# Attention of a streaming encoder step: value products in column strips, bounds inside the projections, the keys' scale moved to the queries

## The reference

```python
h = rms_norm(x, ln1)
proj = h @ w_in
q, k, v, f, xr, yg = jnp.split(proj, SPLITS, axis=-1)
q = rms_norm(q.reshape(B, T, N_HEADS, HEAD_DIM), q_gain)
k = rms_norm(k.reshape(B, T, N_HEADS, HEAD_DIM), k_gain)
...
s = jnp.einsum('bqhd,bkhd->bhqk', q, k) * ATTN_SCALE
s = s + cq - ck                       # cumulative log forget values
s = jnp.where(mask[None, None], s, -jnp.inf)
p = jax.nn.softmax(s, axis=-1)
return jnp.einsum('bhqk,bkhd->bqhd', p, v)
...
mixed = jnp.concatenate([rms_norm(attn, g_ao), rms_norm(lru_out, g_lo)], axis=-1)
x = x + mixed @ w_out
x = x + jnp.square(jax.nn.relu(rms_norm(x, ln2) @ w_up)) @ w_down
```

## Time and profile before

| | us |
|---|---|
| median of 3 runs (1530.29 to 1531.12) | 1530.82 |
| the profiled execution | 1526.91 |
| its span | 1525.2 |
| PE busy | 1423.7 |
| DVE busy | 735.3 |
| ACT busy | 421.4 |
| SP's transfers, share of 16 engines | 21.2% |

### The profile page before, as it was taken

The page is one execution under the profiler, slowest core; times in us unless marked ns, Lnnn a source line. Parts: engine busy times, 40 slices in busy tenths (PEclk is TensorE's granted clock), DMA queues, the critical chain, the costliest instruction groups (busy, mean ns, idle before and its releaser), DMA issues.

```text
span 1525.2 us, 19242 instructions
## 1 busy us (share of the span) xinstructions
PE 1423.7 (93%) x7499; PEld 1232.9 (81%) x7499; DVE 735.3 (48%) x1186; ACT 421.4 (28%) x741; POOL 83.2 (5%) x119
## 2 busy tenths in 40 slices
PE   4979989899898993998999999999999999999997
PEld 3765967859677882887989998999889988999896
DVE  6355364453634646675444454444444444444444
ACT  5124233242334546231312211221112211221110
POOL 2510101101000000000000000000000000000000
PEclk8989999999999996999999999999999999999999
DMA  6023432514222112111111110111011110111004
GB/s 186 8 69 91 127 79 68 143 44 120 65 75 68 30 57 94 60 42 47 60 32 55 41 41 28 55 55 41 19 50 55 41 41 28 55 41 44 24 28 125
DMA packets 133130, 92.87 MB, mean 61 GB/s; under 512 B 22358, under 2 KB 122710, under 8 KB 133076
## 3 DMA queue, kind: packets, MB, share of 16 engines
q1 hardware_dynamic: 133076, 92.14, 21.2%
HBM read 78.24 MB, written 9.68 MB: 58 GB/s over the span
## 4 chain that ended last, share of the span: by engine, by line
PE 88%; DVE 6%; ACT 2%; issue 1%; DMA 1%; POOL 1%; SPq 1%; ACTq 0%; DVEq 0%
PE psum L1473 25%; PE psum L1474 25%; PE psum L1475 25%; PE psum L1694 4%; PE psum L1678 1%; PE psum L1650 1%; DVE tops L1207 1%; PE psum L1681 1%; PE psum L1539 1%; PE psum L1772 1%; POOL rs L694 1%; PE psum L1586 1%; PE psum L1561 1%; DVE cross_qk L1199 0%; PE psum L1793 0%
## 5 line engine op out<-in xcount | busy, mean ns | idle before, releaser
L1441 DVE TENSOR_TENSOR mix<-psum,mix 128x512 f32<-128x512 f32 x288 | 196.4, 690 | 160.4 <-PE psum L1475 160.3
L1473 PE MATMUL psum<-h_hi,wu_hi 128*128 128x384 f32 x768 | 258.9, 337 | 4.2 <-DVE mix L1395 4.2
L1474 PE MATMUL psum<-h_lo,wu_hi 128*128 128x384 f32 x768 | 258.6, 337 | 0.0
L1475 PE MATMUL psum<-h_hi,wu_lo 128*128 128x384 f32 x768 | 258.6, 337 | 0.0
L1473 PE MATMUL psum<-wd_hi,u_hi 128*128 128x512 f32 x576 | 224.2, 389 | 3.6 <-issue 3.6
L1474 PE MATMUL psum<-wd_lo,u_hi 128*128 128x512 f32 x576 | 224.1, 389 | 0.0
L1475 PE MATMUL psum<-wd_hi,u_lo 128*128 128x512 f32 x576 | 224.1, 389 | 0.0
L1473 PEld LDWEIGHTS psum<-h_hi,wu_hi 128*128 128x128 f32 x768 | 144.9, 189 | 4.9 <-issue 4.4
L1474 PEld LDWEIGHTS psum<-h_lo,wu_hi 128*128 128x128 f32 x768 | 144.8, 189 | 0.5
L1475 PEld LDWEIGHTS psum<-h_hi,wu_lo 128*128 128x128 f32 x768 | 144.8, 189 | 0.0
L985 ACT CAST wd_hi<-raw 128x1024 fp32r<-128x1024 f32 x32 | 32.1, 1049 | 401.3 <-PE psum L1475 399.9
(11 more groups left out here) (257 smaller groups left out, 2137.3 us busy)
## 6 DMA issues: line engine op xcount, KB each, us to landing
raw<-in_w_up_dram SPq DMA_DIRECT2D x32, 512.0 KB, 4.6
raw<-in_w_down_dram SPq DMA_DIRECT2D x32, 512.0 KB, 3.3
k_c<-in_cache_k_dram SPq DMA_DIRECT2D x32, 256.0 KB, 3.0
raw<-in_w_in_dram SPq DMA_DIRECT2D x32, 192.0 KB, 4.1
out_dram<-mix SPq DMA_DIRECT2D x9, 512.0 KB
x_in<-in_x_prompt_dram SPq DMA_DIRECT2D x8, 512.0 KB, 4.0
v_c<-in_cache_v_dram SPq DMA_DIRECT2D x16, 256.0 KB, 4.9
kts<-in_cache_v_dram SPq DMA_DIRECT2D x16, 256.0 KB, 3.8
```

The costliest lines, as they stand in the source:

```text
L1441: nc.vector.tensor_tensor(at, psum[:, 4 + 2 * (t % 2) + half, :].rearrange("p (k n) -> p k n", n=P), at, ALU.add).then_inc(y_added, 1)
L1473: nc.tensor.matmul(out, hi(k), r_hi(k), start=first and k == 0, stop=False)
L1474: nc.tensor.matmul(out, hi(k), r_lo(k), start=False, stop=False)
L1475: last = nc.tensor.matmul(out, lo(k), r_hi(k), start=False, stop=end and k == n - 1)
```

## The change

**Steps and strips.** The steps of the two heads alternate. A pair of steps (the same tile of keys, head 0 and 1) has one `values(u)`: two float32 products with 64 columns of values each, into partitions 0 to 63 and 64 to 127 of one bank. The sums of the weights are products of their own, `weight_sums`: for four steps, four products with 32 columns of ones, into four strips of another bank. There are six `pt` buffers instead of three, laid over the buffer of cached values `v_c`, so those are loaded only when a pair's sums are done.

**Bounds.** The order of bounds is a table. Six of them, two turns of tops and the turn of tile 7 stand inside projections 7 and 8 or right behind them; `split_product` is cut into four quarters for that. High parts of tiles 4 and 5 are made after projection 6, of 6 and 7 at projection 8.

**The keys' gain.** The column with which queries are scaled is the product of both gains, so that keys are used without theirs. POOL multiplies the stored keys by the gain (`scale_keys`), after they were turned, and SP's stores wait for that.

**Smaller ones.** Two more small loads at the start; one copy of outputs per half instead of two; denominators copied whole; values are stored by one DMA; `share_out` moves from the projections into the attention.

```diff
 def attention_step(s):
-    if s < 8:
-        return s // 4, 0, s % 4
-    return (s - 8) // 8, 1, (s - 8) % 8
+    return (s % 2, 0, s // 2) if s < 8 else (s % 2, 1, (s - 8) // 2)
...
+    BOUND_AFTER = {(0, 2): ("b", 0, 0), (0, 3): ("b", 0, 1), (1, 0): ("b", 0, 3), (1, 1): ("s", 0, 0), (1, 2): ("b", 1, 0),
+                   (1, 3): ("b", 1, 1), (1, 4): ("s", 1, 0), (0, 5): ("b", 0, 4), (1, 5): ("b", 1, 4), (0, 6): ("b", 1, 5),
+                   (1, 6): ("b", 0, 6), (0, 7): ("b", 1, 6), (1, 7): ("b", 0, 7)}
...
     def bound_bank(hp, t):
-        return 6 + (5 * hp + t) % 2 if t < 4 else 6
+        if t < 4:
+            return 6 + (5 * hp + t) % 2
+        return 2 if (hp, t) in ((0, 4), (0, 5)) else 6
...
             for hp in range(2):
                 sp.dma_start(qgain[hp * DH:(hp + 1) * DH, :], q_gain.rearrange("a d -> d a")).then_inc(small_in, 16)
+                sp.dma_start(kgain_c[hp * DH:(hp + 1) * DH, :], k_gain.rearrange("a d -> d a")).then_inc(small_in, 16)
...
             def keys_out(p, t):
-                sp.wait_ge(qk_ready, NT * p + t + 1)
+                sp.wait_ge(k_scaled, NT * p + t + 1)
...
+                sp.wait_ge(den_done, 6 * p + 6)
+                past_values(p, 0)
                 if not last:
-                    sp.wait_ge(st_done, STEPS * (p + 1))
                     decay_rows(p + 1)
...
+                def scale_keys(t):
+                    pool.wait_ge(qk_turned, NT * p + t + 1)
+                    v = qk[:, t % 3, P:2 * P].rearrange("p (a d) -> p a d", d=DH)
+                    nc.gpsimd.tensor_tensor(v, v, kgain[:, None, :].to_broadcast([P, 2, DH]), ALU.mult).then_inc(k_scaled, 1)
+                    pool.wait_ge(k_scaled, NT * p + t + 1)
                 for t in range(NT):
                     pool.wait_ge(s4_ready, NT * p + t + 1)
                     nc.gpsimd.tensor_tensor(rs4[:, t % 2, :], m4[:, t % 2, :], neg_half[:], ALU.pow).then_inc(rs4_ready, 1)
+                    if t >= 1:
+                        scale_keys(t - 1)
+                scale_keys(NT - 1)
...
                 def exp(s):
                     act.wait_ge(st_done, STEPS * p + s + 1)
-                    if STEPS * p + s >= 3:
-                        act.wait_ge(pv_done, STEPS * p + s - 2)
+                    if s >= 6:
+                        act.wait_ge(den_done, 6 * p + (s - 6) // 4 + 1)
...
-                    d.link(nc.vector.tensor_tensor(v, psum[:, 4 + t % 2, 0:2 * P].rearrange("p (a d) -> p a d", d=DH),
-                                                   rs4[:, t % 2, :, None].to_broadcast([P, 4, DH]), ALU.mult))
-                    nc.vector.tensor_tensor(v[:, 2:4, :], v[:, 2:4, :], kgain[:, None, :].to_broadcast([P, 2, DH]),
-                                            ALU.mult).then_inc(qk_ready, 1)
+                    nc.vector.tensor_tensor(v, psum[:, 4 + t % 2, 0:2 * P].rearrange("p (a d) -> p a d", d=DH),
+                                            rs4[:, t % 2, :, None].to_broadcast([P, 4, DH]), ALU.mult).then_inc(qk_ready, 1)
...
                 for t in range(NT):
+                    if t == 5:
+                        low(0, 0)
+                        low(0, 1)
+                    if t == 7:
+                        bound(1, 1)
+                        bound(1, 2)
+                        bound(1, 3)
+                        bound(0, 4)
+                    if t == 8:
+                        bound(1, 4)
+                        bound(0, 5)
                     mean(t)
+                    if t == 8:
+                        bound(1, 5)
                     norm(t)
...
+                bound(0, 6)
                 low(4, 0)
+                bound(1, 6)
                 low(4, 1)
                 bound(0, 7)
+                bound(1, 7)
+                shift(0, 1)
+                shift(1, 1)
...
+                    for hp in range(2):
+                        r = head_rows(hp)
+                        last = nc.tensor.matmul(psum[r, 4 if qc == 0 else 0, a0 - qc * SPAN:SPAN], v1[:, kt, r],
+                                                pt[:, (s + hp) % 6, 0:a1 - a0], start=kt == 0, stop=kt == 4 * qc + 3)
+                    last.then_inc(pv_done, 1)
+                def weight_sums(kt_of):
+                    for i in range(4):
+                        s = 2 * kt_of + i
+                        _, qc, kt = attention_step(s)
+                        a0, a1 = step_queries(s)
+                        last = nc.tensor.matmul(psum[32 * i:32 * i + 32, 5 if qc == 0 else 1, a0 - qc * SPAN:SPAN], ones_s[:],
+                                                pt[:, s % 6, 0:a1 - a0], start=kt < 2, stop=kt >= 4 * qc + 2)
+                    last.then_inc(den_done, 1)
...
+                meanwhile = {0: (0, 6), 1: (1, 6), 2: (0, 7)}
+                for u in range(STEPS // 2):
+                    if u == 3:
+                        bound(1, 7)
+                    if u < STEPS // 2 - 1 and u != 3:
+                        scores(2 * u + 2)
+                        scores(2 * u + 3)
+                    values(u)
+                    if u % 2 == 1:
+                        weight_sums(u - 1)
+                    if u in meanwhile:
+                        bound(*meanwhile[u])
+                    if u == 3:
+                        turn_qk(NT - 1)
+                        turn_tops(0, 1)
+                        turn_tops(1, 1)
+                        scores(8)
+                        scores(9)
```

More of the change, by code:

```diff
@@ L526, in pair_transfers @@
                 duplicates(p, 0)
-                for t in range(5, NT):
+                for t in range(5, NT - 2):
                     keys_out(p, t)
@@ L1616, in project @@
                         pe.wait_ge(v_done, NT * p + t - 1)
-                    split_product(psum[:, 4 + t % 2, 0:PW3], lambda k: h_hi[:, k, tile(t)], lambda k: h_lo[:, k, tile(t)],
-                                  lambda k: wp_hi[:, k, :], lambda k: wp_lo[:, k, :], KC).then_inc(pair_proj, 1)
+                    for part in range(4):
+                        last = split_product(
+                            psum[:, 4 + t % 2, 0:PW3],
+                            lambda k: h_hi[:, 2 * part + k, tile(t)], lambda k: h_lo[:, 2 * part + k, tile(t)],
+                            lambda k: wp_hi[:, 2 * part + k, :], lambda k: wp_lo[:, 2 * part + k, :], 2, part == 0, part == 3)
+                        if part < 3:
+                            amid(t, part)
+                    last.then_inc(pair_proj, 1)
                 def turn_qk(t):
```

323 lines of the change are left out of this document (159 added, 164 removed).

## The result

The changed kernel takes **1551.55 us** (median of 4 runs, 1548.29 to 1554.80) against 1530.55 us for the kernel before in the same comparison: ratio 1.014, 95% interval 1.0125 to 1.0155. It is slower by 21 us, outside the forecast range of 1504 to 1531. About 7 of these 27.8 us come from the choice of executions: the one of before lies 3.6 us under its median, the one of the changed kernel 3.3 above its own. So against the forecast the medians miss by 31 us, the two profiles by 38.

The account below looks back on a forecast made before the run. Bound by PE, with time to win in the attention. Terms -24.4 (four pairs), +8.1 (clock), +4.7 (pair 0) and +1.2 (start) sum to -10.4 us, from 1530.82 to 1520.4 us; range 1504 to 1531.

Parts of the forecast that it names:

- The stretch of projections: From the streams' scores to the next pair's first score: +2.1 us for bounds, masks and turns, +1.0 for a late key load.
- The `k_c` waits: At turn_past(5), after the streams' scores: its load has 2.4 us of work to cover it instead of 3.4, +1.0 us a pair.
- The clause kept for the range: Loads for turn_past(6) and (7), queued behind 1 MB of values, might come late: +1 us a pair, not in the sum.
- Part A: Attention from the last projection's end to the second query half's first scores: 20.6 us becomes 13.9, -6.7 a pair.
- from there DVE's list runs: After bound(0, 6) at 4.4 us, DVE's maxima and low parts follow without a gap, ending at 10.8 us.
- Part B: Attention from the second query half's first scores to the streams' scores: 23.6 us becomes 21.1, -2.5 a pair.
- The clock: In the attention, PE's waits make its clock fall in three of four pairs, 2.7 us each: +8.1 us.
- Pair 0: Before the first bound: the store of key tile 4 waits for POOL and delays the forget rows, +4.7 us.
- The halves run one after the other: Rival on the attention's value products: 64-column halves run serially, +21 us for four pairs, 1533 to 1539 us; chance 0.13.
- It falls in all four, and the loads come late: Rival: PE's clock falls in all four pairs' attention and loads add up to 4 us, 1523 to 1527 us; chance 0.24.
- DVE clogs the last projections: Rival: maxima delay the norms, PE waits in projections 7 and 8, 1.5 to 2 us a pair, 1526 us; chance 0.10.
- The stores hold up the norms: Rival: norm(t + 3) waits for the late store of tile t's keys, 3 to 5 us a pair, 1530 to 1538; chance 0.05.

Follow-up runs that it names:

- the run with the moved store of pair 0: Changed kernel, with the store of key tile 4 in pair 0 alone placed behind the saving and loading of the forget rows: 1545.23 us.
- the last bound in banks of its own (and the turns moved): Changed kernel with all six edits of lists, POOL's order and turns, plus head 1's bound of tile 7 in the scores' two banks: 1513.80 us.
- DVE's low parts in its idle pieces: The last bound in banks of its own, plus ACT's third cache copy behind the last exponentials and DVE's low parts ahead of maxima: 1507.65 us.
- the version with the loads ahead: Changed kernel, with the load of the second group of cached values ahead of the store of key tile 1 in pairs 1 to 3: 1537.17 us.
- the version with the list edits alone: Changed kernel with three SP list edits: second group's values ahead of key tile 1's store, pair 0's store moved, first group's values behind last key loads: 1527.96 us.
- the version with the first group's values behind the keys: Changed kernel, with the first group's cached values (4 loads) behind the last two loads of keys in SP's list: 1540.26 us.

## Why the prediction was wrong

I forecast 1520.4 and measured 1551.55. In the profiles, where the miss is 38 us, 17 of it lie in the stretch of projections, by a term that I put at nothing (the loads behind the keys' store), and 19 in parts A and B, where the pace of DVE's list, the scores on PE and the base were mis-sized. By its own steps:

**The stretch of projections, forecast +3.1 a pair, measured +8.9.** The failed step is one I did not take. I followed the keys' store to two places: to pair 0's forget rows and to the norm that overwrites the tile (a rival at 0.05). I did not ask what else is queued behind keys_out(p, 1) on SP. There stand the loads of the second group of cached values. The edit that puts them ahead of that store takes back 14.4 us; the profile shows about 3.1 of waiting and 1.8 of clock in each of three pairs. The added terms I did put there were about right: with those loads out of the way and the `k_c` waits down to 1.0 us in all, this stretch is 2.6 us over before (54.0 against 51.45), with 2.1 forecast for bounds and turn. The `k_c` waits, +1.0 forecast, took 1.1 us in pair 2. The clause kept for the range, that the loads for the last turns come late at +1 a pair, was about right for the waits alone: moving the values' loads behind them took 2.3 us of waits away. It left out what goes with the clock, and that edit took back 11.3 us in all.

**Part A, forecast 13.9 us at full clock, measured 16.6 in pair 2.** Of these 2.7 us the clock takes 1.1: at full clock, in the same pair of the run with the moved store of pair 0, part A takes 15.55. In the other 1.65, "from there DVE's list runs" is the step that failed. DVE's timeline in pair 2 of the changed kernel, with the first score at 321.18:

```profile
322.99 0.96 DVE L1232 TENSOR_REDUCE tops<-psum 128x1 f32<-128x768 f32 x1 [0.40 <-PE psum L1694]
...
326.32 1.09 DVE L1232 TENSOR_REDUCE tops<-psum 128x1 f32<-128x896 f32 x1 [2.04 <-PE psum L1694]
...
329.55 1.09 DVE L1232 TENSOR_REDUCE tops<-psum 128x1 f32<-128x896 f32 x1 [0.66 <-PE psum L1694]
...
332.19 1.22 DVE L1232 TENSOR_REDUCE tops<-psum 128x1 f32<-128x1024 f32 x1
334.51 1.23 DVE L1232 TENSOR_REDUCE tops<-psum 128x1 f32<-128x1024 f32 x1 [1.09 <-PE psum L1694]
```

For the first 10 us it is PE that sets the pace, and DVE waits for its bounds (2.04 and 0.66): the maximum of bound(0, 7) ends at 12.2, where I had 10.8. PE stands 1.96 us for it, then starts bound(1, 7), and within that bound its clock falls to the lower level (0.68 over 333.18 to 335.18, 0.50 over the next 2 us). The maxima's turn stands behind values(3), the weight sums and the turn of tile 8 on PE, where I let it follow at once:

```profile
333.47 0.87 PE L1691 MATMUL psum<-KA,QA 128*128 128x512 f32 x2 [1.96 <-DVE tops L1232]
...
335.03 1.07 PE L1751 MATMUL psum<-pt,ones_s 128*32 128x256 f32 x8
...
336.51 0.64 PE L1699 MATMUL psum<-ident,tops 128*4 128x128 f32 x2
337.80 0.47 PE L1720 MATMUL psum<-QA,KA 128*128 128x512 f32 x1 [0.65 <-DVE QA L1236]
```

At full clock that order costs little. From the end of this maximum to scores(8) it is 3.26 us in the run with the moved store of pair 0, against 3.1 forecast, and 4.33 here. So 1.5 us is PE's pace, 0.2 the order behind it, 1.1 the clock. The later versions test the rest: with the last bound in banks of its own (and the turns moved) A takes 14.55 at full clock, with DVE's low parts in its idle pieces 13.9, the forecast's number, but by a version that the change is not.

**Part B, forecast 21.1 us at full clock, measured 22.77.** Here the work was 4.0 us short and the waits 2.4 us too long, so two errors partly cancel. By the chain of waits over pair 2's part B at full clock (331.17 to 353.94 above), scores take 8.95 us where I had 6.4, values 6.9 (6.0), weight sums 3.5 (3.5), turned caches 2.4 (1.8), and waits only 1.0 (3.4). I priced every score product at the 0.23 us of the earlier trace rows. But many first products of a score take 0.43 to 0.48 in this chain, as the one behind a group of values here, and the kernel before already had 7.7 us for the same scores:

```profile
334.01 1.01 PE psum L1743 x4
335.01 0.43 PE psum L1722
```

**The clock, forecast 8.1 us for four pairs, measured about 8.** Against the lengths at full clock (38.32, and 38.52 for pair 3 in the version with the loads ahead) the clock takes 1.5, 2.9, 0.9 and 2.8 us. It fell in all four pairs, behind the wait for bound(0, 7) that I had named, and in three of them stayed down into part B, where I had three falls of 2.7. That the sum agrees is luck, for it changes from one execution to the next: in the profiles of the versions that leave part A and its waits as they are, two, three or four of the four pairs have a fall.

**The base.** I worked on pair 2, whose stretch from the last turn was 44.25 us. It is the longest of the four: the mean from first score to streams is 42.8. That alone is 1.4 us a pair of forecast gain which was never there: 0.7 since the turn and a gap lie outside this stretch, 0.7 since pair 2 stands above the mean. Together a pair has 1.65 (A) + 1.67 (B) + 1.4 (base) = 4.7, which for four is the 19.0 us.

**Strips.** Right in kind: two half-width products run together, 1.01 us a pair of 512 columns where I took 0.93. The weight sums are 1.00 (0.99 forecast):

```profile
340.63 1.01 PE psum L1741 x4
```

A pair of halves is thus 0.15 us longer than the one full-width step of 0.86 in the earlier trace rows, and 0.80 shorter than two steps in a row (1.08 against 1.88 us on the timelines). The Trainium skill, page "TensorEngine Tiling (Array Packing)", section Tiling Modes, says that different tiles can execute matmuls in parallel, and the two kernels agree with it.

**Pair 0.** Forecast +4.7 for the store and +1.2 for the gain column; PE's first bound moved from 91.74 to 99.19, +7.45. Right in mechanism, 1.5 us short: the wait itself grew by 5.0 (4.17 to 9.13), and PE came to it 2.5 later, where 1.2 was forecast (x's fourth load went out 1.06 later, 12.44 against 11.38). The first score moved by 9.8, with 8.0 forecast.

**The rivals.** "The halves run one after the other": no, though products in a row cost about what it said. "It falls in all four, and the loads come late" had the clock right for this execution and the right kind of cause, but the loads it meant were the keys', with 3.9 us of waits in all, and not the values'. "DVE clogs the last projections": no, one wait of 0.41 us a pair in front of a bound. "The stores hold up the norms": no wait of a norm for a store was found; stores held up loads, which I had not listed. No rival gave a time over 1539.

## What to carry to other kernels

When a wait in a DMA queue's list gets a later due time, walk down the list behind it, line by line, and compare each load's new issue with the moment its reader is ready; here one store that waits for POOL in place of DVE moved loads that the change did not touch by 8.5 us. Scaling in place makes the store wait for the last reader of the unscaled tile; moving the scale up in its engine's list did nothing for it here. Measure a base over all repetitions of a loop: the one pair that was taken as the example was the longest. And price the clock by the same stretch at full clock in another run: mean clock times length counts time in which PE waits anyway (in pair 2's A and B it gives 1.6 us, the comparison 0.9).

## What the runs showed of the hardware

- The granted clock differs between runs of one kernel, and the time with it. The changed kernel's four are 1548.3, 1548.5, 1554.6 and 1554.8 us, with mean clocks of 0.969, 0.969, 0.960 and 0.958, and the version with the list edits alone spread from 1521 to 1535. The Trainium skill, page "TensorE: Matmul & The Clock Gate", Part 1, says that how many matmuls run at the low clock differs from run to run of one kernel; the spread of these runs agrees. For such a kernel one profile is not enough to price a change of 5 us.
- One and the same wait can be followed by a fall of the clock or not. Waits of PE of 2.8 to 3.2 us in the projections were followed by a fall that took 1.8 us, about 4 us near the lower level, in all three pairs of the changed kernel and of the version with the moved store of pair 0. In the version with the first group's values behind the keys it fell behind the wait of 3.00 us, and not behind those of 2.83 and 2.82.
- The same holds for the wait of 1.97 us in part A. The clock fell behind it in all four pairs of the changed kernel's profile; in pair 2 of the version with the moved store of pair 0, the same code with the same wait, A and B have a clock of 1.00.
- Half-width strips of 512 columns run together. With the sums in groups of their own, values and sums together have 78.5 us of busy PE where the values with their sums had 84.1 (sums over the forms of L1741 and L1751, and of L1694 before). Against the kernel before, the strips so win 6 us of PE's busy time in the whole program, no more (both sums hold some time at the lower clock).
